# A hybrid attention, recurrence and mixture-of-experts step: expert products on 32-column tiles, down projection ahead of the turns, recurrence sums regrouped

## The reference

```
proj = rmsnorm(x) @ w_in
x += concat(attention, recurrence) @ w_o
h = rmsnorm(x)
out = sum over e of gates[:, e] * ((silu(h @ w_gate[e]) * (h @ w_up[e])) @ w_down[e])
x += out; y = rmsnorm(x)
```

## Time and profile before

| | us |
|---|---|
| median of 3 runs (lowest, highest) | 506.78 (503.93, 507.75) |
| the profiled execution's own time | 506.22 |
| its span in the profile | 504.4 |
| TensorE busy | 455.1 |
| mixture of experts, first gate product to last down product | 319.1 to 469.9 |

### The profile page before, as it was taken

How to read it: one execution, slowest core, us unless ns; L and a number is a source line. 1 busy time by engine, 2 the same in 40 slices (tenths; PEclk the granted TensorE clock), 3 DMA queues, 4 the chain that set the end, 5 groups by cost and what they waited for, 6 DMA issues and landing times.

```text
span 504.4 us, 7576 instructions
## 1 busy us (share of the span) xinstructions
PE 455.1 (90%) x2901; PEld 309.3 (61%) x2901; DVE 250.0 (50%) x597; ACT 156.9 (31%) x355; POOL 91.7 (18%) x156
## 2 busy tenths in 40 slices
PE   6999899999999999999999989899999999999200
PEld 6879799887988687778887769243433333333000
DVE  4777615487487263965765576343411111211086
ACT  6574630564246445641412230111111111111021
POOL 5238001120000000010000123110222111111153
PEclk9999999999999999999999895799999999999855
DMA  8904402104004920331101099978989999950494
GB/s 302 216 7 169 166 9 99 69 1 166 2 2 92 242 71 0 101 88 43 42 1 64 25 387 403 360 293 321 399 343 411 424 399 420 390 201 32 144 317 167
DMA packets 31822, 93.18 MB, mean 185 GB/s; under 512 B 8968, under 2 KB 12176, under 8 KB 25648
## 3 DMA queue, kind: packets, MB, share of 16 engines
q1 hardware_dynamic: 27728, 82.81, 45.6%
q0 software_dynamic: 4064, 9.97, 5.3%
HBM read 85.75 MB, written 11.80 MB: 193 GB/s over the span
## 4 chain that ended last, share of the span: by engine, by line
PE 80%; DVE 9%; DMA 5%; ACT 3%; issue 1%; SPq 1%; POOL 1%; POOLq 0%; DVEq 0%; ACTq 0%
PE ps L2085 17%; PE ps L2065 9%; PE ps L1735 8%; PE ps L1737 7%; PE ps L1736 7%; PE ps L1947 3%; PE ps L2040 3%; PE ps L1948 3%; PE ps L1949 3%; DMA pair<-y_pairs 3%; PE ps L1972 2%; PE ps L1890 1%; PE ps L1887 1%; PE ps L1781 1%; ACT s_buf L929 1%
## 5 line engine op out<-in xcount | busy, mean ns | idle before, releaser
L2085 PE MATMUL ps<-we_gu,xT 128*32 128x512 f32 (+1 forms) x640 | 87.6, 612 | 1.2 <-issue 1.2
L2085 PEld LDWEIGHTS ps<-we_gu,xT 128*32 128x32 f32 (+1 forms) x640 | 25.7, 118 | 54.1 <-issue 51.1
L1735 PE MATMUL ps<-hT_hi,w_hi 128*128 128x288 f32 x160 | 48.5, 303 | 1.7 <-DVE w_lo_q L1110 0.8
L2065 PE MATMUL ps<-we_d,hhT 128*32 128x512 f32 (+1 forms) x320 | 43.7, 596 | 1.1 <-DVE hhT L1651 1.1
L1642 DVE TENSOR_TENSOR hh<-sg,ps 128x256 f32<-128x256 f32 x12 | 5.1, 421 | 73.6 <-ACT sg L1056 73.6
L1735 PE MATMUL ps<-w_hi,hT_hi 128*128 128x512 f32 x96 | 39.0, 407 | 0.0
L1736 PE MATMUL ps<-w_lo,hT_hi 128*128 128x512 f32 x96 | 37.5, 391 | 0.0
L1735 PEld LDWEIGHTS ps<-hT_hi,w_hi 128*128 128x128 f32 x160 | 30.1, 188 | 5.0 <-issue 2.6
L1056 ACT ACTIVATE sg<-ps 128x256 f32<-128x256 f32 x12 | 4.6, 383 | 86.2 <-PE ps L2085 86.2
L856 ACT ACTIVATE w_hi<-ring,g_col 128x512 fp32r<-128x512 f32 (+1 forms) x48 | 28.8, 680 | 0.0
L1737 PE MATMUL ps<-hT_hi,w_lo 128*128 128x288 f32 x96 | 28.3, 295 | 0.0
(11 more groups left out here) (389 smaller groups left out, 979.8 us busy)
## 6 DMA issues: line engine op xcount, KB each, us to landing
we_gu<-in_w_gate SPq DMA_DIRECT2D x16, 1024.0 KB, 9.6
we_gu<-in_w_up SPq DMA_DIRECT2D x16, 1024.0 KB, 12.2
we_d<-in_w_down SPq DMA_DIRECT2D x16, 1024.0 KB, 8.7
ring<-in_w_in SPq DMA_DIRECT2D x4, 2048.0 KB, 7.9
pair<-y_pairs SPq DMA_DIRECT2D x8, 512.0 KB, 7.9
ring<-in_w_in SPq DMA_DIRECT2D x3, 1024.0 KB, 7.9
x_first<-in_x_p SPq DMA_DIRECT2D x4, 512.0 KB, 9.6
x<-in_x_p SPq DMA_DIRECT2D x4, 512.0 KB, 3.9
```

The costliest lines, as they stand in the source:

```text
L1735: pe.matmul(out, stationary[0], moving[0], start=c == 0, stop=False)
L2065: last = pe.matmul(ps[cols, 4 + 2 * (b % 2) + half, :], hhT[:, f, cols], we_d[u][:, f, 512 * half:512 * half + 512], start=f == 0, stop=f ...
L2085: last = pe.matmul(ps[cols, 0, :], xT[:, c, cols], we_gu[u][:, :, c, :], start=c == 0, stop=c == KC - 1)
```

## The change

Three things change. `tiles_of` gives tiles of 32 columns in every block, so block 1 makes four products where it made two. In the experts' blocks the order changes on three engines: TensorE makes the down product of the block before directly behind gate and up, and then the ten transposes; ScalarE and VectorE empty `y` before they copy `xT`. TensorE waits for VectorE's half of `xT` only when it comes to step 4 of 8. In `sums` the full-width products of the four heads come first, the first of them alone with the start flag, and the half-width products of all heads behind them.

```diff
 def tiles_of(b):
-    runs = runs_of(b)
-    width = QUAD if any(n % (2 * QUAD) for _, n, _ in runs) else 2 * QUAD
-    return [(at + d, width, u) for at, n, u in runs for d in range(0, n, width)]
+    return [(at + d, QUAD, u) for at, n, u in runs_of(b) for d in range(0, n, QUAD)]
...
                     act.activation(sg[:, :], ps[:, 0, 0:FE], ACT.Silu).then_inc(silu_ready, 1)
-                    take_x(s + 1)
                     if b:
                         take_y(i, b - 1)
                     elif i is not first:
                         take_y(i - 1, PER - 1)
+                    take_x(s + 1)
...
                     dve.tensor_tensor(hh[:, :], sg[:, :], ps[:, 0, FE:2 * FE], ALU.mult).then_inc(hh_ready, 1)
-                    take_x(s + 1)
                     if i is first and b == 0:
                         weights()
                     if b:
                         take_y(i, b - 1)
                     elif i is not first:
                         take_y(i - 1, PER - 1)
+                    take_x(s + 1)
...
                 for h in range(BH):
                     cols = slice(h * BK, (h + 1) * BK)
-                    terms = []
+                    pe.matmul(ps[0:r, 5, cols], aT[0:r, h, 0:r], vf[0:r, t, cols], start=h == 0, stop=True,
+                              skip_group_check=h > 0)
+
+                for h in range(BH):
+                    cols = slice(h * BK, (h + 1) * BK)
                     for c in range(r // CHUNK):
                         before = s_sample if t == NT - 1 else St[(2 * t + c) % 3]
+                        rows = slice(c * CHUNK, (c + 1) * CHUNK)
                         if 2 * t + c:
-                            terms.append((c, before))
-                    pe.matmul(ps[0:r, 5, cols], aT[0:r, h, 0:r], vf[0:r, t, cols], start=True, stop=True)
-                    for c, before in terms:
-                        rows = slice(c * CHUNK, (c + 1) * CHUNK)
-                        last = pe.matmul(ps[rows, 5, cols], qex[:, h, rows], before[:, cols], start=False,
-                                         stop=True, skip_group_check=True)
+                            last = pe.matmul(ps[rows, 5, cols], qex[:, h, rows], before[:, cols], start=False,
+                                             stop=True, skip_group_check=True)
...
                     pe.wait_ge(xT_act, s + 1)
-                    pe.wait_ge(xT_dve, s + 1)
...
                     for c in range(KC):
+                        if c == KC // 2:
+                            pe.wait_ge(xT_dve, s + 1)
...
                     last.then_inc(gu_ready, 1)
-                    pe.wait_ge(gathered[following], 16 * (i + (b + 1) // PER + 1))
-                    turn_half(following, 0, x_turned_a)
-                    turn_half(following, 1, x_turned_b)
                     if b:
                         down(i, b - 1)
                     elif i is not first:
                         down(i - 1, PER - 1)
+                    pe.wait_ge(gathered[following], 16 * (i + (b + 1) // PER + 1))
+                    turn_half(following, 0, x_turned_a)
+                    turn_half(following, 1, x_turned_b)
```

## The result

| | before | after |
|---|---|---|
| median, us (lowest, highest) | 506.36 (503.93, 507.75) | 493.81 (491.68, 495.03) |
| runs | 4 | 4 |
| the profiled execution | 506.22 | 491.68 |
| its span | 504.4 | 489.9 |
| last down product starts | 466.2 | 453.0 |

A forecast was written before the change was run, and what follows sets the result against it. TensorE, busy 90% of the span and 80% of the chain that ended last, was taken to bound the kernel. From the median 506.78, 4.5 (recurrence) and 2.7 (experts' stage), together 7.2, gave 499.6 us; range 496 to 503.5.

The forecast's parts named there:

- that rival: Experts' loop: the weights come late, so the experts' gain stops at some 1 us and the kernel takes 501.3; chance 0.08.
- the rival in which it stays behind: Recurrence: its gain does not arrive, up to 4 us stay behind, and the kernel takes 504; chance 0.07.
- the rival with transposes and wait: Experts' blocks: TensorE's clock falls at the ten transposes and the wait, some 1.7 us each fall; chance 0.04.
- 0.34 for a round trip of widths: Recurrence, tile 0: changing between half-width and full-width products costs 0.14 and 0.20; three of four go, saving 1.0 us.
- the pace of 0.11: Recurrence: half-width products in a row follow each other at 0.11 us; at 0.16, tile 0 would save 0.73.
- 0.15 a boundary: Experts' loop: two changes of width save 0.36 a block, a new wait gives back 0.21; eight boundaries make 1.2 us.
- `y` decides: ScalarE in the loop: the copy of y, free at T + 0.82, sets when the xT copy starts, not the transposes at T + 0.75.
- T: Experts' loop: the start of the transposes; the next gate was put at T + 1.52, without the wait at T + 1.31.
- The rival in which the wait eats the gain: Experts' loop: the new wait loses 8 x 0.19, only the recurrence counts, and the kernel takes 502.3; chance 0.14.
- That is 0.8 earlier, but part of it lies in the half-clock stretch there; I take 0.5.: First turn, block 0: gate and up can start at 318.32 instead of 319.12, behind ScalarE's half; 0.5 us gained.
- the 0.4 behind it: First turn: TensorE's 0.39 us of idle time ahead of block 1, behind VectorE's half, goes; 0.4 us gained.
- The fall at 280 may move or vanish, 1.7 us either way.: Window 280 to 284, granted clock 0.57: the stretch costs 1.7 us and may move or vanish.

## Why the prediction was wrong, point by point

**What held.** TensorE bounds the kernel, and what it saved reached the end. The weights never came late: no wait for `we_gu` shows, so that rival falls. The sums' gain arrived whole (4.94), so the rival in which it stays behind falls as well. The changed order did not slow the clock in the loop, so the rival with transposes and wait falls too:

```profile
350.00:440.00 90.00, 89.59 (x808) 33.54 (x804) 16.37 (x31) 12.27 (x24) 19.51 (x32) 1.00 0.95 382
```

**The sums.** Summed with 0.34 for a round trip of widths I had 4.85 and took 4.5; 4.94 came. Taking off 0.35 for doubts was not needed: the pace of 0.11 was right. Tile 0 gave 1.0 (3.01 to 2.00) and tile 4 0.84 (2.88 to 2.04), both as worked out.

**The loop.** Forecast 0.15 a boundary, measured 0.23. The change of width was priced right: down and the two transposes got 0.34 shorter, where "0.36" was forecast. What was given back was not. Without any new wait a block would take 12.11 - 0.36 = 11.75; it takes 11.84 in two of three blocks, so 0.09 is given back there and not 0.21, and 12.03 only at the turn of the loop. "`y` decides" was the wrong step: on ScalarE the copy of `xT` starts 0.75 behind the start of the transposes with `y` ahead of it or behind it, so the transposes alone set its start. The prediction also counted T from two rows that lie 0.07 apart, the timeline's start of the transposes for the copy (T + 1.52) and the chain's for the case without the wait (T + 1.31). By the chain's, TensorE starts at T + 1.33 in two of three blocks (391.02 to 392.35), 0.05 behind the copy's end, and at T + 1.52 at the turn of the loop, 0.24 behind it (380.27 to 380.51). The rival in which the wait eats the gain fails by the same rows. It would have been true with the early wait (12.42 a block).

**The step that failed: the clock.** The mechanism that was forecast, shorter work on TensorE, came as described (7.2 forecast, some 8 measured); what is missing lies in the granted clock. It was in the prediction twice, and neither time as something to be gained.

- "That is 0.8 earlier, but part of it lies in the half-clock stretch there; I take 0.5." I priced the earlier start of the first gate product, and not what it does to the product. The low level does not end at a fixed time, after which everything is as before. Over the kernels with 30 filler products, the first stage takes 10.4 to 12.0 us in the seven profiles with the early wait and 8.5 to 10.1 in the seven with the late one; the means are 11.5 and 9.4, although the idle time itself is only 0.6 to 0.8. All fourteen have 2.0 to 3.5 us of idle time ahead of the transposes, where TensorE waits for the gather (2.8 and 2.7 on the mean), so it is the later idle time that sets the two groups apart. The later wait alone gave 2.7 us by the median (1.0 to 3.8) where this step and the 0.4 behind it had 0.9: 1.8 us too little, give or take 1.4.
- "The fall at 280 may move or vanish, 1.7 us either way." It was put into the range and not into the sum. The prediction saw that it lies "behind the narrow sums and the 20-column routing products", and the change takes the alternation out of the sums. So it should have been asked whether the fall goes. It goes, in all nine profiles with new sums. With seven falls in eight profiles of old sums this is some 7/8 x 1.6 = 1.4 us, an estimate from these counts. The sums alone gave 7.2 us, 2.3 more than their work; the interval of that run takes in 0 and 1.4 alike.

With these two, 7.2 + 1.8 + 1.4 = 10.4; the sums' 0.4, the first turn's 0.13 and the loop's 0.64 make 11.6 of the 12.5. The one that is left is within what medians of four runs leave open. In the profiled execution the clock was also already up at the first gate product, 1.0 us more than in the second profile; no run explains when that is so.

The mean clock of all executions gives a second estimate. Every run lists its span and mean granted clock, and span x (1 - clock) is what the low clock takes away, in idle time too. On the mean this is 26.3 us in the kernel before (71 executions of the experiments) and 22.8 in the changed one (5), 3.5 less, give or take 1.5; the rest of the span falls from 477.3 to 469.1, by 8.2, where 7.2 was forecast for all. It is 25.1 with the sums alone (4) and 25.1 with the later wait alone (12), but 26.5 with the experts' part alone (10), no less than before. So the clock's part of the gain, some 3 to 4 us, comes out of the profiles and of these means alike; how it divides between the two sources is known only roughly.

**What stays open.** That falls come where old sums and routing products follow each other, and not with new sums, is shown by where they lie and how often; why, is not. TensorE reads as busy throughout the stretches in which it falls. The Trainium skill, "TensorEngine Tiling (Array Packing)", section "Key Properties", says that changing the tiling mode drains TensorE, and "TensorE: Matmul & The Clock Gate", in the section on a second failure mode of the gate, tells of short idle times between groups of matmuls that make the clock go up and down. The 0.14 to 0.18 us at each change of width in these rows would fit both; neither page is shown to be the cause by a run here, and that such gaps lower the clock was not isolated.

## What to carry to other kernels

Ahead of a stage that starts at the low clock, an idle microsecond cost more than itself here (0.6 to 0.8 us went with 2.1): look at the granted clock of the stretch and price what the stage would take at the high level. When products of different shape share an accumulation, group them by shape; each change here cost 0.14 to 0.2 us, and the alternation, with routing products behind it, went with falls of the clock that cost another 1.6 each. When a reordering puts a copy right ahead of its consumer, let the consumer wait for the half it needs first: here the same reordering is worth 0.23 us a block with the late wait and costs 0.3 with the early one.

## What was unexpected of the hardware

The falls of the granted clock come with TensorE busy for all of the 4.00 us and cost about 1.6 us each (1.60 between the two profiled executions); for the same code they are in four of six profiles, and move (237, 259.8, 280). The first gate product of the same instructions takes anything from 7.07 to 10.00 us. Going from 64 to 32 columns costs a down product as much as going from 32 to 64 (3.57 and 3.58 us against 3.43), and as much as going from a transpose to 64 columns (3.58) or to 32 (3.57, at 376.37 in the same chain).
